# Up product of the MLP by seven block products of 256 columns, with the sums of weight blocks made by GpSimd

## The reference

```python
D_FF = 4 * D_MODEL            # 4096, D_MODEL = 1024

        h2 = rmsnorm(x, pre_norm_mlp[l])
        y = jnp.square(jax.nn.relu(h2 @ w_up[l])) @ w_down[l]
        x = x + rmsnorm(y, post_norm_mlp[l])
```

## Time and profile before

| | |
|---|---|
| median of 3 runs | 929.79 us (929.73 to 930.12) |
| span of the profiled execution | 928.3 us |
| TensorE busy | 919.0 us (99%) |
| weight loads of TensorE busy | 750.9 us (81%) |
| VectorE busy | 657.3 us (71%) |
| ScalarE busy | 483.0 us (52%) |
| GpSimd busy | 113.8 us (12%) |
| DMA | 97.01 MB, mean 104 GB/s |

### The profile page before, as it was taken

How to read it: one execution, slowest core, us unless ns; L and a number is a source line. 1 busy time by engine, 2 the same in 40 slices (tenths; PEclk the granted TensorE clock), 3 DMA queues, 4 the chain that set the end, 5 groups by cost and what they waited for, 6 DMA issues and landing times.

```text
span 928.3 us, 13427 instructions
## 1 busy us (share of the span) xinstructions
PE 919.0 (99%) x5050; PEld 750.9 (81%) x5050; DVE 657.3 (71%) x1163; ACT 483.0 (52%) x880; POOL 113.8 (12%) x122
## 2 busy tenths in 40 slices
PE   9999999999999999999999999999999999999997
PEld 8778777777898777777777889988888888888886
DVE  7668759888749787766564751879556857775787
ACT  6455346355555355644543324578646435634554
POOL 2003202431040001100000213000000000000015
PEclk9999999999999999999999999999999999999999
DMA  7322112112232411212212355433633453363245
GB/s 252 96 87 68 47 47 80 58 46 80 91 114 88 168 46 55 77 54 78 65 50 69 114 181 182 159 91 90 225 100 95 146 160 100 82 203 115 68 100 151
DMA packets 28048, 97.01 MB, mean 104 GB/s; under 512 B 3280, under 2 KB 4240, under 8 KB 27728
## 3 DMA queue, kind: packets, MB, share of 16 engines
q1 hardware_dynamic: 24864, 85.04, 28.2%
q0 software_dynamic: 2544, 6.62, 3.9%
q10 hardware_dynamic: 576, 4.49, 1.3%
HBM read 85.65 MB, written 4.19 MB: 97 GB/s over the span
## 4 chain that ended last, share of the span: by engine, by line
PE 85%; DVE 9%; ACT 3%; issue 2%; DVEq 0%; ACTq 0%
PE PB L446 13%; PE PB L448 12%; PE PB L447 12%; PE PB L1046 5%; PE PB L1047 5%; PE PB L1048 5%; PE PB L653 4%; PE PB L690 3%; PE PB L668 2%; DVE wl L1559 2%; PE PB L893 2%; PE PB L894 2%; PE PB L895 2%; PE PB L491 2%; PE PB L487 2%
## 5 line engine op out<-in xcount | busy, mean ns | idle before, releaser
L446 PE MATMUL PB<-hh,wh 128*128 128x512 f32 x576 | 234.9, 408 | 0.0
L448 PE MATMUL PB<-hh,wl 128*128 128x512 f32 x576 | 224.7, 390 | 0.0
L447 PE MATMUL PB<-hl,wh 128*128 128x512 f32 x576 | 224.5, 390 | 0.0
L1559 DVE TENSOR_TENSOR wl<-raw,wh 128x1024 fp32r<-128x1024 f32 (+2 forms) x114 | 143.1, 1255 | 70.4 <-ACT wh L1071 70.1
L1071 ACT ACTIVATE wh<-raw 128x1024 fp32r<-128x1024 f32 (+2 forms) x114 | 116.4, 1025 | 71.2 <-PE PB L491 14.0
L446 PEld LDWEIGHTS PB<-hh,wh 128*128 128x128 f32 x576 | 108.1, 188 | 28.1 <-issue 6.2
L448 PEld LDWEIGHTS PB<-hh,wl 128*128 128x128 f32 x576 | 108.1, 188 | 23.3
L447 PEld LDWEIGHTS PB<-hl,wh 128*128 128x128 f32 x576 | 108.3, 188 | 22.7 <-issue 1.9
L1238 ACT ACTIVATE S<-S,sm 128x256 f32<-128x256 f32 (+3 forms) x96 | 50.6, 529 | 105.0 <-DVE sm L1662 80.7
L1071 ACT ACTIVATE wh<-AR 128x1024 fp32r<-128x1024 f32 x56 | 59.0, 1057 | 53.0 <-PE PB L1048 51.0
L1559 DVE TENSOR_TENSOR wl<-AR,wh 128x1024 fp32r<-128x1024 f32 x56 | 68.0, 1221 | 17.6 <-ACT wh L1071 17.4
(11 more groups left out here) (400 smaller groups left out, 1825.6 us busy)
## 6 DMA issues: line engine op xcount, KB each, us to landing
AR<-in_dn SPq DMA_DIRECT2D x40, 512.0 KB, 4.4
raw<-in_upe SPq DMA_DIRECT2D x28, 512.0 KB, 3.5
raw<-in_w2g SPq DMA_DIRECT2D x16, 512.0 KB, 3.4
raw<-in_w1e SPq DMA_DIRECT2D x10, 512.0 KB, 3.4
raw<-in_w1q SPq DMA_DIRECT2D x8, 512.0 KB, 3.5
raw<-in_woab SPq DMA_DIRECT2D x8, 512.0 KB, 3.5
AR<-AR POOLq DMA_DIRECT2D x8, 512.0 KB, 4.5
raw<-in_w2e SPq DMA_DIRECT2D x5, 512.0 KB, 4.3
```

The source lines that it names most:

```text
L446: e.matmul(bank[:], a[:, col(k)], xa[:, k, :], start=k == 0, stop=False)
L447: e.matmul(bank[:], a[:, col(k)], xb[:, k, :], start=False, stop=False)
L448: i = e.matmul(bank[:], b[:, col(k)], xa[:, k, :], start=False, stop=k == 7)
L1559: e.tensor_tensor(wl[c % 3][:, 0:n], raw_of(c), wh[c % 3][:, 0:n].bitcast(F32), ALU.subtract).then_inc(*up("lo", c))
```

## The change

In quarters 1 to 3 the up product of four hidden tiles (a group `g`, two per quarter) becomes seven products of blocks, in place of eight. Its weights are split in four blocks A11, A12, A21, A22 of 512 input channels by 256 hidden channels, the features in four blocks of 512 channels by 256 tokens. Each product `r` (1 to 7) has one piece of weights, 24 matmuls of 256 columns: 2 hidden tiles, 4 tiles of channels, 3 matmuls. Three PSUM banks hold running sums: products 1, 6, 7 and 4 follow each other in one bank, 5 and 3 in another, 2 in a third, and ScalarE copies the bank out (`kept`) before the next product is added to it.

- GpSimd sums the weights' blocks: `chain_first` (A21 + A22, by an accumulating DMA), `chain_second` (its sum plus A11), `chain_third` (plus A12), `other_sum` (a DMA). It takes over `second` and `fourth` of the down weights from VectorE, and squares parts of the hidden features (`odd_square`, `last_square`).
- The features' blocks are mixed once, in the down part of quarter 0: GpSimd scales `x` in place, `X[:, k]`, and makes four sums of 128 x 1024; ScalarE and VectorE make high and low parts in the place of `X`, of the upper halves of `hh`/`hl`, and in `MT`. `x` itself is saved in memory before (`keep2`) and fetched back after the last block product (`back2`). The sums of squares of `x` go two to a beat.
- The order of a quarter, `OPENING`, mixes block products with the last two down pieces of the quarter before and the first two of its own; then ten more down pieces follow: 28 beats. ScalarE's and VectorE's work is put into these beats by hand.
- The weights of the up product are laid out anew on the host (`ub`), and the scratch of GpSimd's DMAs is set to 2048.

```diff
+OPENING = (("p", 0, 1), ("d", 12), ("p", 0, 5), ("d", 13), ("p", 0, 6), ("p", 0, 2), ("p", 0, 3), ("p", 0, 7),
+           ("p", 1, 5), ("p", 1, 1), ("p", 0, 4), ("p", 1, 6), ("p", 1, 2), ("p", 1, 3), ("p", 1, 7), ("d", 0),
+           ("p", 1, 4), ("d", 1))
...
+            def block_product(q, g, r):
+
+                c = product(q, g, r)
+                a, b = wh[c % 3], wl[c % 3]
...
+                kept = {6: 1, 7: 6, 4: 7, 3: 5}.get(r)
+                more = kept is not None
+                e.wait_ge(*to("lo", c))
+                if before:
+                    e.wait_ge(*to(*before))
+                if kept:
+                    e.wait_ge(*to("pc", q, g, kept))
+                if (q, g) == (1, 0) and r > 3:
+                    e.wait_ge(*to("fl", r))
+                for j in range(2):
+                    o = bank[:, 256 * j:256 * j + 256]
+                    for k in range(4):
+                        w = slice(512 * j + 128 * k, 512 * j + 128 * k + 128)
+                        high, low = factor(r, k)
+                        first, last = r in (1, 2, 5) and j == k == 0, j == 1 and k == 3
+                        e.matmul(o, a[:, w], high, start=first, stop=False, skip_group_check=more)
+                        e.matmul(o, a[:, w], low, start=False, stop=False, skip_group_check=more)
+                        i = e.matmul(o, b[:, w], high, start=False, stop=last, skip_group_check=more)
...
             for q in range(4):
-                for m in range(4 if q == 0 else 0, 8):
-                    bank, before = tenant(6 + m % 2 if q else (6, 1, 7, 2)[m - 4], "re", q, m)
-                    tile(upper(q, m), bank, before, hh, hl)
...
+                for kind, *x in OPENING if q else ():
+                    if kind == "p":
+                        block_product(q, *x)
+                    else:
+                        down(q - 1 if x[0] > 11 else q, *divmod(x[0], 2))
...
+            def kept(q, g, r):
+
+                e.wait_ge(*to("gemm", product(q, g, r)))
+                if (q, g) > (1, 0):
+                    e.wait_ge(*to({1: "t0", 6: "tw1", 7: "bl2", 5: "v22"}[r], *((q, 0) if g else (q - 1, 1))))
...
+                e.activation(tmp[{1: 0, 6: 1, 7: 2, 5: 3}[r]][:], bank[:], ACT.Copy).then_inc(*up("pc", q, g, r))
...
+            def mix(q, g, i):
+
+                if i == 0:
+                    e.wait_ge(*(to("tw3", q, 0) if g else to(*summed(q - 1, 5, 0))))
+                    e.wait_ge(*to("rb", q, g, 0))
+                    e.wait_ge(*to("u12", q, g))
+                    x, y = tmp[1], tmp[0]
...
+                e.tensor_tensor(MIX[i][:], x[:], y[:], ALU.subtract).then_inc(*up(f"t{i}", q, g))
...
+                    if b == 9:
+                        mix(q, 0, 0)
+                    if b == 11:
+                        mix(q, 0, 1)
+                        mix_low(q, 0, 0)
+                    if b == 13:
+                        mix_low(q, 0, 1)
+                    if b == 16:
+                        mix(q, 1, 0)
...
+                    if c + 2 < len(PLAN):
+                        lo(c + 2)
...
+                    if b == 10:
+                        mix(q, 0, 2)
+                    if b == 12:
+                        mix(q, 0, 3)
+                        hidden_low(q, 0, 2)
...
+            def chain_second(q, g):
+
+                w = WE[1 - g][:]
+                e.wait_ge(semaphore(f"chain{g}"), 16 * q)
+                e.wait_ge(semaphore(f"first{g}"), 16 * q)
+                e.wait_ge(*to("lo", product(q, g, 5)))
+                e.tensor_tensor(w, w, WE[g][:], ALU.add).then_inc(*up("wc2", q, g))
...
+            def odd_square(q, g):
+
+                u = tmp[1][:]
+                e.wait_ge(*to("v12", q, g))
+                e.tensor_scalar(u, u, 0.0, None, ALU.max).then_inc(*up("r12", q, g))
+                e.wait_ge(*to("r12", q, g))
+                e.tensor_tensor(u, u, u, ALU.mult).then_inc(*up("u12", q, g))
...
+            for q in range(1, 4):
+                chain_second(q, 0)
+                chain_third(q, 0)
+                chain_first(q, 1)
+                chain_second(q, 1)
+                odd_square(q, 0)
+                other_sum(q, 1)
+                last_square(q, 0)
+                chain_third(q, 1)
+                second(q, 0)
+                second(q, 1)
+                sum_a(q, 0)
+                odd_square(q, 1)
+                last_square(q, 1)
+                sum_a(q, 1)
+                fourth(q, 0)
+                fourth(q, 1)
+                if q < 3:
+                    chain_first(q + 1, 0)
+                    other_sum(q + 1, 0)
```

More of the change, by code:

```diff
@@ new lines, in pe, with down @@
+            down_bank = {}
+            def down(q, n, jj):
+                if jj == 0:
+                    down_bank[n] = [tenant(DOWN_BANKS[n][s], *summed(q, n, s)) for s in range(2)]
+                    if (q, n) == (0, 6):
+                        e.wait_ge(*to("xs", 2, 7))
+                        sums(2, 2)
+                    if q == 0 and n == 2:
+                        e.wait_ge(*to("tw", q, 3, 1))
+                    if q and n == 5:
+                        e.wait_ge(*to("bl2", q, 1))
+                        for i in (2, 3):
+                            e.wait_ge(*to(f"tw{i}", q, 1))
+                c = piece(q, n, jj)
+                a, b = wh[c % 3], wl[c % 3]
+                e.wait_ge(*to("lo", c))
+                if q:
+                    ready = {0: "bl0", 1: "bl1", 2: "tw1", 3: "tw0", 4: "tw2", 6: "tw3"}.get(n)
+                    if ready:
+                        e.wait_ge(*to(ready, q, jj))
+                for j in (2 * jj, 2 * jj + 1):
+                    w = slice(512 * (j % 2), 512 * (j % 2) + 512)
+                    if q == 0 and n < 2:
+                        e.wait_ge(*to("bl", q, j, n))
+                    for s in range(2):
+                        bank, before = down_bank[n][s]
+                        if j == 0:
+                            e.wait_ge(*to(*before))
+                        high, low = features(n, j, s)
+                        e.matmul(bank[:], high, a[:, w], start=j == 0, stop=False)
+                        e.matmul(bank[:], low, a[:, w], start=False, stop=False)
+                        x = e.matmul(bank[:], high, b[:, w], start=False, stop=j == 3)
+                x.then_inc(*up("gemm", c))
@@ new lines, in pe @@
+            got = [tenant(DOWN_BANKS[6][s], "ye", 3, 6, s) for s in range(2)]
+            e.wait_ge(*to("lo", piece(3, 6, 0)))
+            e.wait_ge(semaphore("back2"), 16)
+            turned_x(2, (7, 2))
+            turned_x(3, (6, 3))
+            e.wait_ge(*to("lo", piece(3, 6, 1)))
+            e.wait_ge(*to("tw3", 3, 1))
+            for s in range(2):
+                bank, before = got[s]
+                e.wait_ge(*to(*before))
+                for j in range(4):
+                    jj, w = j // 2, slice(512 * (j % 2), 512 * (j % 2) + 512)
+                    a, b = wh[piece(3, 6, jj) % 3], wl[piece(3, 6, jj) % 3]
+                    high, low = features(6, j, s)
+                    e.matmul(bank[:], high, a[:, w], start=j == 0, stop=False)
+                    e.matmul(bank[:], low, a[:, w], start=False, stop=False)
+                    x = e.matmul(bank[:], high, b[:, w], start=False, stop=j == 3)
+                x.then_inc(*up("gemm", "last", s))
@@ L1054, in act @@
+            turned_x(0, (4, 5))
+            turned_x(1, (7, 2))
         def act(e):
@@ new lines, in chain_third, with other_sum @@
+            def chain_third(q, g):
+                w, c = WE[1 - g][:], product(q, g, 2)
+                e.wait_ge(*landed(c))
+                e.wait_ge(*to("wc2", q, g))
+                e.wait_ge(*to("lo", product(q, g, 6)))
+                e.tensor_tensor(w, w, raw_of(c), ALU.add).then_inc(*up("wc4", q, g))
+            def other_sum(q, g):
+                if g:
+                    e.wait_ge(*to("wc2", q, 1))
+                    e.wait_ge(*to("lo", product(q, 1, 1)))
+                    w, a = WE[1][:], A21
+                else:
+                    c = product(q, 0, 7)
+                    e.wait_ge(*landed(c))
+                    w, a = raw_of(c), A11
+                e.dma_start(w, block(q, g, a), accum_op=ALU.add).then_inc(semaphore(f"third{g}"), 16)
@@ new lines, in pool @@
+            first, last = slice(0, 256), slice(256, 512)
+            for jj in range(2):
+                second(0, jj)
+            for jj in range(2):
+                sum_a(0, jj)
+            for jj in range(2):
+                fourth(0, jj)
+            chain_first(1, 0)
+            other_sum(1, 0)
+            e.wait_ge(semaphore("keep2"), 16)
+            for k in range(8):
+                e.wait_ge(*to("xq", 2, k))
+                e.tensor_scalar(X[:, k, :], X[:, k, :], pcol(P_PREF + k), None, ALU.mult).then_inc(*up("fx", k))
@@ L2485, in sync @@
                             load_down(name, jj, q + 1)
-                    for m in range(2, 8):
```

(9 more changed lines are left out.)

563 lines of the change are left out of this document (408 added, 155 removed), and 11 rows, old and new, of the table SIGNALS.

## The result

| | before | after |
|---|---|---|
| median | 929.76 us (929.37 to 930.12, 4 runs) | 978.47 us (978.17 to 978.73, 4 runs) |
| span of the profiled execution | 928.3 us | 977.0 us |
| mean granted clock of TensorE | 1.0 | 0.983 |

The ratio is 1.052, 95% interval 1.051 to 1.054: slower by 48.7 us, where 15 were forecast (945, range 924 to 961). The direction was right, the size outside the range.

The account below looks back on a forecast made before the run. The kernel before was taken as bound by the sum of TensorE's instructions (busy 919.0 of 928.3 us). 929.8 - 9.6 gain + 3 x 8 stalls + 1 for quarter 0 = 945 us, range 924 to 961.

Parts of the forecast that it names:

- The gain on TensorE: Up product, quarters 1 to 3: 336 steps of 0.120 us replace 192 of 0.2267; 3.2 us a quarter, 9.6 in all.
- the port: Shared SBUF access: VectorE operations with two SBUF inputs and GpSimd's exclude each other; 69 of 78.4 us a quarter.
- the port-free chain before p7: Group 1's product 7: without port conflicts it comes out at 39.9 us, undisturbed beats 40.0, so no slack.
- the walk: Quarter's queues followed in diff order, port first come, first served: stalls 5.7 us up to p7, 10.3 in all.
- the signs: Profile if right: TensorE under 96% busy, waits for `wl` and `pc`, low parts 1.6 to 3.5 us, 0.12 steps, quarters 83 to 88.
- Quarter 0, "0 to 4 us, I take 1": Quarter 0's down part: four GpSimd feature sums in a row hold the port from low parts; 1 us taken.
- Of the second part I take half.: Stalls behind p7, 4.6 us a quarter in the walk, halved; 8 us a quarter taken in all, bounds 4 and 13.
- The end, "I take 0": After the last block product: X fetched back late could cost 0 to 5 us at the end; 0 taken.
- The one-input price, 0.62: GpSimd's one-input operation of 512 columns, such as clamps at zero, taken as 0.62 us, between 0.61 and 1.28.
- The conflicts stay in the slack: Rival: port conflicts stall TensorE only 0 to 2.5 us a quarter, 920 to 927.7 us; chance 0.21.
- GpSimd's chain is late: Rival: semaphores and DMA sums make group 1's p5 wait, 1.6 us a quarter more, 960 to 970 at worst; chance 0.08.
- Weight loads as the bound: Rival: 256-column matmuls bound by weight loads at 0.19 us, 64 us, +20 a quarter; chance under 0.01.

Follow-up runs that it names:

- with fills: Changed kernel with GpSimd's sums, clamps, squares and scalings in the MLP replaced by about equally long memsets that read nothing; 928.2 us.
- the halts in the kernel before: Kernel before, TensorE halted in down products behind chains of GpSimd memsets only it waits for; 942.9 us with shorter halts, 968.0 us with longer ones.
- the version that moved three of the jobs away: Changed kernel with squares and scaling on ScalarE, `second` on VectorE, `fourth` later, some mixes one or two beats earlier; 942.4 us.
- the last kernel: Kernel with the new order, plus GpSimd's first two result scalings earlier, quarter 0's `fourth` later, quarter 1's feature lows a beat later; 931.5 us.
- the one with the new order: Three-moves version reordered: quarter 0's `fourth` on VectorE, quarter 1's root earlier, both `second` before chain sums, last DMA sums before GpSimd's end scaling; 935.1 us.

## Why the prediction missed

**What held.** The gain on TensorE: from 711.88 to 713.92 us the changed kernel makes 17 steps of 256 columns, 0.120 each, and with fills 3.1 us of waits are left in the block products. (One side sum is off: 144 instructions at 13 ns are 1.9 us, not 2.2; the gain doesn't hang on it.) That the port is the resource that decides, and what is on it (two SBUF inputs yes, PSUM form no). The price of a sum of 1024: 2.35 forecast, the shortest in the trace are 2.4, and their means of 2.5 to 3.1 hold waiting. The places: p6, p3 and p7 of group 1, d2 and d3 (d1 had no stall), and the port-free chain before p7 that has no slack. Per quarter the walk gave 5.7 us up to p7 and 4.6 behind it, 10.3. In quarter 1 the trace has 2.65, 2.3 and 1.4 up to p7, and 0.6 and 3.35 behind it, which is 10.3, and 1.4 more for `root`; quarters 2 and 3 have 10.3 and 9.6. That the sums agree is luck in part: one price was wrong, and the single stalls don't agree (p6 0.8 forecast and 2.65 measured, p7 3.1 and 1.4). Of the signs, low parts up to 3.4 us, the waits for `wl` and `pc` and the step of 0.12 came as written; the quarters took 91.6 to 100.5 us where 83 to 88 were named.

**The steps that failed,** by size; the first four make 32.1 of the 33.5 us from 945 to 978.5:

1. *Full granted clock, read for the kernel before, was carried over to the changed one without being said.* 12.4 us. The sum prices a stall at its own length. Eight of the ten stalls of 2.3 us and more cost some 1.55 us on top, and the halts in the kernel before, where nothing else was changed, show that the stall is enough (six of seven of 2.75 us and more). The traces of before had no such stall, so the price couldn't be read; but the assumption could have been named, with both levels as the bounds of the price: at half clock the distance between matmuls was 0.43 us for 512 columns and 0.22 for 256, twice that at full clock.
2. *Quarter 0, "0 to 4 us, I take 1".* Measured 9.4, outside its own bounds: 8.4 us. Two mistakes. The down sums of quarter 0 that GpSimd takes over were put with those "hidden before", although a transfer to the port's other user isn't hidden; they hold the low part at 637 us (3.39 for 1.22) and TensorE for 3.0 us, and with the sums back on VectorE that stall is gone. And the eight scalings took 2.18 us each, not 0.62 to 1.28; on ScalarE they are 4.6 us cheaper, half clock included.
3. *"Of the second part I take half."* 7.6 us over three quarters (31.6 for 24). The argument was that a stall lets VectorE catch up. The stalls at d3 (3.35, 2.7 and 3.35 us, for 2.5 in the walk) show no such relief. That GpSimd's queue is pushed back by the same stalls and meets VectorE again behind them is a reading of the order, which no run tests alone. The walk's own sum, 3 x 10.3 = 30.9, was the better number.
4. *The end, "I take 0".* 3.7 us. The term was put down to X fetched late (`back2`), and no transpose waited for that. What came late were GpSimd's scaled results: VectorE's `final` waits for them, and TensorE's last transposes for `final`. The run with fills has the same loss, 4.0 us, so the reading sums aren't its cause; with the first two results earlier in GpSimd's queue (the last kernel, against the one with the new order) 2.5 us came back.
5. *The one-input price, 0.62.* Wrong by a factor of two to three: the shortest clamp in the trace took 1.49 us, most 1.8 to 1.9. The bounds were drawn from copies of 32 rows and from two-input operations, on the belief that one input can't be dearer than two. It is part of why the stall of p6 was 2.65 and not 0.8; its whole worth can't be told apart, but the squares' move to ScalarE gave 21.8 us, the largest of the three.

1.4 us stay unexplained; the fifth has no sum of its own, it lies in the others. **The rivals.** "The conflicts stay in the slack" failed at the place that spoke against it, p7; it would have needed the version that moved three of the jobs away. "GpSimd's chain is late" was not what happened to the changed kernel: the waits name `lo` and `hidden_low`; it is what happened when a DMA made the second sum. "Weight loads as the bound" is out: 0.120 per step wherever the clock was full.

**The range** ended at 961 because its upper end was built from one kind of cost, more stalls. Costs of another kind (clock, quarter 0, the end) were taken at nothing or near it.

## What to carry to other kernels

Before work is given to an idle GpSimd, list VectorE's operations with two SBUF inputs that someone waits for: every GpSimd operation that reads SBUF is added to that queue, and back-to-back ones on either side are one block. Here a step that made TensorE wait some 3 us in a row mostly cost half as much again by the clock, and behind halts of 1.0 to 2.4 us the clock stayed full, so several short ones were cheaper than one long. A gain of 1% in matmuls is soon eaten: here it was 9.6 us, and the best order found is still 1.5 us slower than the kernel before.

## What the runs showed of the hardware

- GpSimd's one-input `tensor_scalar` on 128 x 512 takes 1.5 to 2.2 us, a square (the same tile as both inputs) 1.04, a multiply of two tiles 1.29 and a memset 0.53 to 0.57. The Trainium skill, GPSIMD Engine Reference, section 3.1, has a measured figure for the two-input form; no run here shows why one input should be dearer.
- The port is kept across operations: GpSimd's two sums, 5.00 us, kept a VectorE operation of 0.7 us out from start to end (6.54 for the pair of additions), and VectorE's three kept GpSimd's sum waiting (5.50 for 2.4). The Trainium skill, SBUF — State Buffer, "SBUF: two separate sides", has the shared pair held for the whole of one instruction by whoever starts first; what happens between two that follow each other isn't in that rule, and in these two places the other side got no turn. In the kernel before it did once, at 161.87 us, so it isn't always so.
- The clock falls a little after the work has resumed as well: behind a halt ending at 733.9 + 3.7 = 737.5 us it was half from 738.8 on; at the one ending at 753.65 it was half already.
